# Key and value products of the next head pair in six runs instead of singly between the 64x64 units

## The reference, cut to what matters

```python
def step(s, inp):
    w_t, k_t, v_t, kk_t, kka_t = inp[:5]
    sa = jnp.einsum('bhvk,bhk->bhv', s, kk_t)
    s = (s * w_t[:, :, None, :] - sa[..., None] * kka_t[:, :, None, :]
         + v_t[..., None] * k_t[:, :, None, :])
    y = jnp.einsum('bhvk,bhk->bhv', s, inp[5]) if len(inp) == 6 else None
    return s, y
```

## Time and profile before

| | before |
|---|---|
| median of three runs | 2094.38 us (2093.79 to 2096.22) |
| the profiled execution | 2096.83 us |
| its span in the profile | 2095.0 us |
| TensorE busy | 1978.0 us (94%) |
| VectorE busy | 607.6 us (29%) |
| ScalarE busy | 485.1 us (23%) |
| GpSimd busy | 104.1 us (5%) |
| bytes moved | 489.70 MB, mean 234 GB/s |

### The profile page before, as it was taken

How to read it: one execution, slowest core, us unless ns; L and a number is a source line. 1 busy time by engine, 2 the same in 40 slices (tenths; PEclk the granted TensorE clock), 3 DMA queues, 4 the chain that set the end, 5 groups by cost and what they waited for, 6 DMA issues and landing times. The chain is left out here.

```text
span 2095.0 us, 46331 instructions
## 1 busy us (share of the span) xinstructions
PE 1978.0 (94%) x20126; PEld 1160.5 (55%) x20126; DVE 607.6 (29%) x1299; ACT 485.1 (23%) x861; POOL 104.1 (5%) x136
## 2 busy tenths in 40 slices
PE   3589999999999999999859999999999999999997
PEld 1158787777778777778344344434444344434442
DVE  2135444535363535453241111111111111111111
ACT  1123333332423242434111111111111111111111
POOL 0001111101020202020000000000000000000000
PEclk9689999999999999999959999999999999999998
DMA  6922111111110202020238999999999999999995
GB/s 254 375 64 66 42 36 43 46 33 56 33 56 23 66 13 76 13 72 3 94 158 324 422 422 422 422 422 422 422 422 422 422 421 422 422 422 422 422 422 233
DMA packets 75328, 489.70 MB, mean 234 GB/s; under 512 B 9616, under 2 KB 10688, under 8 KB 21168
## 3 DMA queue, kind: packets, MB, share of 16 engines
q1 hardware_dynamic: 75056, 487.43, 57.9%
q0 software_dynamic: 128, 0.11, 0.0%
HBM read 486.46 MB, written 1.05 MB: 233 GB/s over the span
## 5 line engine op out<-in xcount | busy, mean ns | idle before, releaser
L1368 PE MATMUL PS<-raw,hgT 128*64 128x512 f32 x2120 | 471.8, 598 | 0.0
L1368 PEld LDWEIGHTS PS<-raw,hgT 128*64 128x64 f32 x2120 | 147.5, 137 | 298.0 <-issue 297.7
L1414 PE MATMUL PS<-raw,actT 128*64 128x512 f32 x1056 | 232.2, 592 | 0.0
L701 PEld LDWEIGHTS PS<-raw 64*64 64x64 f32 x6144 | 191.8, 135 | 45.2 <-issue 45.2
L701 PE MATMUL PS<-raw 64*64 64x64 f32 x6144 | 213.2, 220 | 0.0
L670 PE MATMUL PS<-arena 128*128 128x256 f32 x640 | 166.5, 399 | 10.6 <-ACT arena L514 10.6
L636 PE MATMUL PS<-arena 128*128 128x256 f32 x512 | 170.6, 424 | 0.0
L1414 PEld LDWEIGHTS PS<-raw,actT 128*64 128x64 f32 x1056 | 75.9, 137 | 150.7 <-issue 150.7
L1353 PEld LDWEIGHTS PS<-take,MT 128*128 128x128 f32 x1088 | 127.3, 196 | 31.3 <-issue 26.8
L1483 DVE TENSOR_SCALAR back<-cst,now 128x128 f32<-128x128 f32 x66 | 19.9, 343 | 428.4 <-PE PS L1419 428.4
L1353 PE MATMUL PS<-take,MT 128*128 128x64 f32 x1088 | 132.0, 281 | 4.4 <-DVE take L1464 4.4
(11 more groups left out here) (297 smaller groups left out, 2019.6 us busy)
## 6 DMA issues: line engine op xcount, KB each, us to landing
raw<-in_w_exp SPq DMA_DIRECT2D x397, 1024.0 KB, 16.4
arena<-in_w_blk SPq DMA_DIRECT2D x67, 512.0 KB, 3.6
raw<-in_w_ada SPq DMA_DIRECT2D x24, 1024.0 KB, 17.9
arena<-in_w_out SPq DMA_DIRECT2D x8, 512.0 KB, 3.5
arena<-in_lora_up SPq DMA_DIRECT2D x8, 192.0 KB, 3.9
cst<-in_consts SPq DMA_DIRECT2D x1, 1330.5 KB, 5.9
arena<-in_ctx SPq DMA_DIRECT2D x2, 512.0 KB, 7.6
xl<-in_x SPq DMA_DIRECT2D x2, 512.0 KB, 8.9
```

Of the source, the lines that this page charges most:

```text
L701: ins = mm(out[H[h], c, :], lhsT[H[h], c, :], rhs[H[h], c, :], start=True, stop=True)
L1368: ins = mm(PS[H[h], GU + g, :], hgT[:, s, :], raw[:, s, cols], start=False, stop=s == KT - 1, skip_group_check=True)
L1414: ins = mm(PS[H[m], Y, :], aT[:, q, H[h]], raw[:, KT + q, cols], start=q == 0 and h == 0, stop=q == 3 and h == 1, skip_group_check=True)
```

## The change

The 32 `ahead` products of the next pair are no longer placed one after a unit. They are done in six runs: 0 to 7 after both `G1` units, 8 to 15 after both `G4` units, 16 to 19 before `Y8`, 20 to 23 before `TP`, 24 to 27 before `Y64`, 28 to 31 before `WT`. `var_and_bonus(j - 1)` moves from behind `G2` to behind the run 8 to 15, directly ahead of the `AT` turns, and VectorE's `spread(j - 1)` moves from behind `G2` to behind `G4`. ScalarE's program, the transfers and all products are as before.

```diff
+            RUNS = {"Y8": (16, 20), "TP": (20, 24), "Y64": (24, 28), "WT": (28, 32)}
             for j in range(KT):
+
+                def run(start, end):
+
+                    for n in range(start, end):
+                        ahead(j + 1, n)
...
                 for d in (0, 1):
                     waits(d, "feat_dn")
                     unit("G1", "c", d, BE[d], AL[d])
-                    ahead(j + 1, d)
+                run(0, 8)
                 if j:
                     mean(j - 1)
...
                     unit("G2", "a", d, AL[d], BE[d])
-                    ahead(j + 1, 2 + d)
-                if j:
-                    var_and_bonus(j - 1)
...
                     unit("G3", "b", d, KA[d], AL[d])
-                    ahead(j + 1, 4 + d)
...
                     ins.then_inc(S["G4_mm"], 1)
-                    if d == 0:
-                        ahead(j + 1, 6)
+                run(8, 16)
+                if j:
+                    var_and_bonus(j - 1)
                 for d in (0, 1):
                     waits(d, "G2_ev")
                     turn("AT", bank["a"][d], AL[d])
...
                     unit("N2P", "b", d, NF[d], NP[d])
-                    ahead(j + 1, 7 + d)
...
                     unit("N2F", "c", d, NP[d], NF[d])
-                    if d == 0:
-                        ahead(j + 1, 9)
...
+                    if job in RUNS:
+                        run(*RUNS[job])
                     if job == "TP" and j < KT - 1:
                         squares(j + 1)
...
                             unit(job, b, d, lhsT[d], rhs[d])
-                        m = 2 * n + d
-                        if m % 4 < 3 and 10 + m - m // 4 < 4 * KT:
-                            ahead(j + 1, 10 + m - m // 4)
...
                     step(tt(NP[d], bk("a", d), k2(f"nP{d}"), ALU.mult), S["G2_ev"])
-                if j:
-                    spread(j - 1)
...
                     step(tt(RK[d], bk("c", d)[:, NL:NC, :], kl, ALU.mult), S["G4_ev"])
+                if j:
+                    spread(j - 1)
```

More of the change, by code:

```diff
@@ L771, in _ @@
                         turn(job, bank[b][d], src[d])
-                for n, (job, b, lhsT, rhs, need) in enumerate((
+                for job, b, lhsT, rhs, need in (
                     ("Y2", "c", Q0P, YY, ("N2F_ev", "y1_dn")),
@@ L788, in _ @@
                     ("U0", "b", YY, X, ()),
-                )):
+                ):
+                    if job in RUNS:
+                        run(*RUNS[job])
                     if job == "TP" and j < KT - 1:
```

## The result

| | before | after |
|---|---|---|
| median | 2095.3 us (2093.79 to 2097.26, four runs) | 2046.34 us (2045.83 to 2046.54, four runs) |
| the profiled execution | 2096.83 us | 2046.28 us |
| its span | 2095.0 us | 2044.5 us |
| TensorE busy | 1978.0 us | 1919.9 us |
| VectorE, ScalarE busy | 607.6, 485.1 us | 608.0, 485.1 us |

The ratio is 0.9765, 95% interval 0.9749 to 0.9782: faster by 49 us, or 2.3%. TensorE's busy time fell by 58 us with the same 20126 instructions, while the other engines' work is unchanged.

What follows compares the result with a forecast made beforehand. TensorE's queue was taken to bound the mixing stage. Fewer switches, less ScalarE waits and the moved step's delay, gave 52.3 us: the profiled execution 2096.8 to 2044.5, the median 2094.4 to 2042; range 2035 to 2054.

Steps and rivals of the forecast that it cites:

- (a): Whole kernel: the summed gains and waits hold as forecast, median 2042 us; chance 0.85.
- Switches removed: Pairs 0 to 6: 27 fewer full-array stretches between 64x64 units, 0.35 us each, 9.5 us a pair; pair 7 0.35.
- The cover: `AT` turns to second `N4F`: without seven singles TensorE waits for ScalarE's copies, 1.72 us in each of pairs 0 to 6.
- The moved step: `var_and_bonus` before the `AT` turns: ScalarE's copy chain starts 0.45 us late (bounds 0.4 and 0.5), pairs 1 to 7.
- Other steps, at nothing: Remaining steps, such as `Y4`, `N8P`, `N8F`, `Y8`, `TP`, `Y64` and `WT`: no added cost.
- The nearest to late: VectorE's norm of the next keys before the first `Y64` eviction: 1.2 us of slack left.
- The sum: Gains of 7.36 us in each of pairs 1 to 6, 7.8 in pair 0, 0.3 in pair 7; together 52.3.
- (b): Evictions late at eight further dependent steps, 0.49 us each, 3.9 a pair, 27 in all: 2069 us; chance 0.08.
- (c): Switch costs no less in a run, 0.35 us belonging to each product; only waits added: 2109 us; chance 0.02.
- (d): Idle time in the packed stretch drops the clock to 1.2 GHz, 9.6 us a pair: 2109 us; chance 0.05.
- The sign named for (d): A granted clock below 1.00 between 170 and 980 us would show the clock rival.
- a run of eight was to take 3.4 us: Pair 3: run of eight products, first record to the following `mean`, takes 3.4 us.

Runs made afterwards that it cites:

- the products in the units' own form: Key and value products as 64x64 products: singles in the kernel before, runs in the changed kernel; pair 3, `vt` to `receptance`, 60.20 and 62.12 us.
- runs of two: Kernel before with its products in sixteen runs of two at the odd-numbered singles' places, `var_and_bonus` where it was: 2057.99 us, ratio 0.9817.
- the move alone: Kernel before with `var_and_bonus` and `spread` moved as in the change, the single products kept in place: 2096.00 us, ratio 0.9998.
- the kernel with fewer stretches: Changed kernel with products regrouped beside existing full-array work, three full-array stretches between `vt` and `receptance` instead of seven: 2029.67 us, ratio 0.9686.
- the kernel with the runs alone: Changed kernel with `var_and_bonus` and `spread` put back behind `G2`: 2044.45 us, ratio 0.9758.

## Why the prediction was right, point by point

It said 2042 us, 2035 to 2054; measured were 2046.34. Forecast (a) held: TensorE's queue got shorter and the ScalarE chain took a quarter of that back (2.18 of 9.17 us per pair).

- **Switches removed.** The mechanism is shown by the products in the units' own form. The term was slightly too large: 0.35 us was put on each switch, and three measurements give 0.34 (0.341 in runs of two, 0.343 with the form kept; in the change 6.99 us of gain plus 2.18 of waits over 27 stretches, 0.340). Over 27 stretches and seven pairs that is 2 us. What the switch consists of stays open.
- **The cover.** 1.72 us plus 0.45 were forecast for pairs 1 to 6, 2.17; the stretch from the `AT` turns to the second `N4F` is 13.61 us instead of the 11.43 that TensorE needs, 2.18. Three waits of that chain are visible, and filling them gave 2.17 back. The two terms apart were less exact than their sum: with the step not moved the stretch is 13.08 us, 1.65 over the 11.43 where 1.72 was forecast, and the moved step adds 0.53 where 0.45 was, outside its bounds of 0.4 and 0.5.
- **The moved step.** ScalarE's first `AT` copy comes 1.23 us after the turns' start; 1.2 was forecast. Without the move it comes after 0.69 us (491.57 against 490.88), not the 0.75 read in pair 7, where the turns begin a full-array stretch. That its cost counts only where the cover is gone is shown by the move alone, which cost nothing.
- **Other steps, at nothing.** No other wait appeared in the kernel after. The nearest to late was named rightly: VectorE's norm ends at 529.37 (528.62 + 0.75) and the first `Y64` subtraction starts at 530.62, waiting 1.24 for TensorE; 1.2 was forecast. It became the bound in the kernel with fewer stretches.

```profile
528.62 0.75 DVE L911 SCALAR_TENSOR_TENSOR raw<-arena,par,raw 128x512 f32<-128x512 f32 x1
530.62 0.69 DVE L1021 TENSOR_TENSOR raw<-raw,PS 128x512 f32<-128x512 f32 x1 [1.24 <-PE PS L707]
```

- **The sum.** Pairs 1 to 6 gained 7.00 us each (102.13 for 109.13; 7.36 forecast), pair 0 7.5 (7.8), pair 7 0.24 (0.3): 49.8 us together where 52.3 were forecast. The profiled execution went from 2096.83 to 2046.28, 50.6 us, so 0.7 us net were gained outside these stretches, and that part is luck: the `vt` turns of pair 0 came 1.95 us earlier (169.49 for 171.44), in a stage in which nothing was edited (in the kernel with the moved step alone they came at 171.28, in runs of two at 170.29) and where the granted clock was 0.91 instead of 0.83 from 140 to 160 us, and behind the scan of pair 7 some 1.1 us were lost to the clock (below). The other part of the 4.3 us by which the median is above 2042 is the anchor: I took the gain off a median of three that lay 2.5 us below its own profiled execution, while the median after lies at its profiled one. With more runs the median of before was 2095.1 to 2096.3. The profiled execution's own 2044.5 was the better figure to give.
- **The rivals.** (b) shows no trace: ScalarE's quarter copies are the only new cause of a wait. It was priced too low, though. It took the 0.49 us of the view for the cost of a wait; the two of pair 7 also stand 1.64 us apart instead of 0.933 (956.26 to 957.90), 0.71 each, which would have made it some 40 us and not 27, 2082 us. (c) is refuted by the runs of two and by 3.56 us for eight products. (d) is refuted for the stretch that it was about: 17.4 us of idle time in 810, the new waits of it 0.71 us each, and a granted clock of 1.00 from 160 to 970 us. The sign named for (d), a clock below 1.00 before 980 us, was there all the same, from 972.4 us, but behind the last scan and not in the packed stretch. The Trainium skill's section on a second failure mode ("TensorE: Matmul & The Clock Gate") tells of a kernel in which short pauses between groups of matmuls let the clock swing; the pauses of this packed stretch did not.

A slip in the sizes that I gave as signs: a run of eight was to take 3.4 us up to `mean`, and took 3.56, since a part of the step into the full form lies in its first product (the same run directly behind the `vt` transposes takes 3.46, 469.61 to 473.07 in the kernel with fewer stretches); the sum had it in the switch.

## What to carry to other kernels

Where work in a 64x64 form and full-array work share TensorE, count the changes of form and not the instructions, and put full-array products next to transposes or other full-array work that is there anyway. Then look at what the scattered products had covered: walk the packed order with each engine's chain of evictions, and put products back into the one stretch where another engine is slower. A slack of about a microsecond in that walk is worth writing down, because the next packing step spends it.

## What the runs showed of the hardware

A change from the 64x64 form to the full array and back costs 0.34 us between float32 matmuls at the full clock, whether one full-array product stands in between or two; the mean over stretches in the changed kernel, with runs of four and eight, is the same. It costs nothing if the product in between has the units' form. The Trainium skill ("TensorEngine Tiling (Array Packing)", Key Properties) says that a change of tiling mode drains TensorE. The traces are in line with it, in that the first weight load behind a change starts no earlier than its matmul (514.61, 515.24); they do not show the drain itself, and how much of the 0.34 us is drain and how much unhidden load stays open.

The clock also took something back. At the end of pair 7's scan the two products of `var_and_bonus` took 1.17 and 1.06 us in the kernel after, against 0.70 and 0.59 before:

```profile
972.36 1.17 PE L724 MATMUL PS<-raw,cst 128*128 128x256 f32 x2 [1.07 <-ACT raw L571]
973.33 1.06 PE L725 MATMUL PS<-raw,cst 128*128 128x256 f32 x2
```

The granted clock is 1.00 up to 972.4 us and 0.50 from 972.5 to 981 us, and a clock at half is in keeping with their length. `project` then began 9.05 us after the first of them, where it was 8.15 before (972.36 to 981.41, 1024.11 to 1032.26), so this cost 0.9 us, and its first eight records took 5.83 us to the next product for 5.62. It is not shown to be an effect of the change: in the kernel with the runs alone, whose last scan is the same, the two products took 0.70 and 0.59.
